# Low parts of every fourth gate and up weight chunk: a ScalarE activation and an accumulating DMA instead of a VectorE subtraction

## What is computed

```python
def swiglu(h, w_gate, w_up, w_down):
    return (jax.nn.silu(h @ w_gate) * (h @ w_up)) @ w_down

x = x + multiscale_pool_mixer(rms_norm(x, pool_norm), pool_w, pool_scale)   # layer 0
x = x + mla_layer_mixer(rms_norm(x, attn_norm), ...)                        # layer 1
x = x + swiglu(rms_norm(x, ffn_norm), w_gate, w_up, w_down)                 # both
```

## Time and profile before

| | |
|---|---|
| device time, 2 runs | 1771.51 and 1771.73 us, median 1771.62 |
| span of the profiled execution | 1769.1 us |
| TensorE matmul busy | 1761.5 us (100%) |
| VectorE busy | 1130.7 us (64%) |
| ScalarE busy | 914.3 us (52%) |
| GpSimd busy | 113.1 us (6%) |
| weights loaded by SyncE's queue | 327.03 MB, 55.5% of the 16 DMA engines' span |
| granted TensorE clock, mean | 0.999 |

### The profile page before, as it was taken

The page is one execution under the profiler, slowest core; times in us unless marked ns, Lnnn a source line. Parts: engine busy times, 40 slices in busy tenths (PEclk is TensorE's granted clock), DMA queues, the critical chain, the costliest instruction groups (busy, mean ns, idle before and its releaser), DMA issues.

```text
span 1769.1 us, 29325 instructions
## 1 busy us (share of the span) xinstructions
PE 1761.5 (100%) x10438; PEld 1564.0 (88%) x10438; DVE 1130.7 (64%) x1460; ACT 914.3 (52%) x1176; POOL 113.1 (6%) x132
## 2 busy tenths in 40 slices
PE   9999999999999999999999999999999999999998
PEld 6888888888888888889999888888888888888887
DVE  5766666556666666678997776666655566666554
ACT  6666664334444453456775466666533344445433
POOL 2100000000000001124111420000000000000000
PEclk9999999999999999999999999999999999999999
DMA  7555556545555566545445555555665455556642
GB/s 282 195 188 190 189 197 229 191 155 177 190 190 190 190 223 196 175 152 160 148 137 179 190 184 191 189 188 188 230 200 166 162 190 190 190 190 222 227 146 72
DMA packets 86017, 328.79 MB, mean 186 GB/s; under 512 B 9680, under 2 KB 11088, under 8 KB 85840
## 3 DMA queue, kind: packets, MB, share of 16 engines
q1 hardware_dynamic: 85680, 327.03, 55.5%
q10 hardware_dynamic: 288, 1.11, 0.2%
HBM read 326.01 MB, written 2.10 MB: 185 GB/s over the span
## 4 chain that ended last, share of the span: by engine, by line
PE 100%; DVE 0%; issue 0%; DVEq 0%; ACT 0%; POOL 0%; POOLq 0%
PE ps L435 58%; PE ps L436 31%; PE ps L505 2%; PE ps L443 1%; PE ps L445 1%; PE ps L444 1%; PE ps L799 1%; PE ps L798 1%; PE ps L797 1%; PE ps L633 0%; PE ps L632 0%; PE ps L631 0%; PE ps L685 0%; PE ps L493 0%; PE ps L705 0%; PE ps L706 0%
## 5 line engine op out<-in xcount | busy, mean ns | idle before, releaser
L1238 DVE TENSOR_TENSOR w_lo<-raw,w_hi 128x1024 fp32r<-128x1024 f32 (+2 forms) x564 | 736.0, 1308 | 419.1 <-ACT w_hi L850 416.9
L435 PE MATMUL ps<-xg,w_hi 128*128 128x512 f32 x2880 | 999.7, 390 | 0.0
L850 ACT ACTIVATE w_hi<-raw 128x1024 fp32r<-128x1024 f32 (+2 forms) x565 | 630.9, 1120 | 548.9 <-PE ps L436 533.2
L436 PE MATMUL ps<-xg,w_lo 128*128 128x256 f32 x2880 | 812.1, 282 | 0.0
L435 PEld LDWEIGHTS ps<-xg,w_hi 128*128 128x128 f32 x2880 | 540.5, 188 | 113.5 <-DVE w_lo L1238 0.3
L436 PEld LDWEIGHTS ps<-xg,w_lo 128*128 128x128 f32 x2880 | 544.3, 189 | 0.1
L435 PE MATMUL ps<-act,w_hi 128*128 128x512 f32 x1320 | 458.0, 390 | 0.0
L436 PE MATMUL ps<-act,w_lo 128*128 128x256 f32 x1320 | 372.2, 282 | 0.0
L435 PEld LDWEIGHTS ps<-act,w_hi 128*128 128x128 f32 x1320 | 247.7, 188 | 51.9
L436 PEld LDWEIGHTS ps<-act,w_lo 128*128 128x128 f32 x1320 | 249.5, 189 | 0.0
L1318 DVE TENSOR_TENSOR sums<-ps,cross 128x512 f32<-128x512 f32 x88 | 60.8, 691 | 93.1 <-ACT cross L928 93.1
(11 more groups left out here) (200 smaller groups left out, 1240.2 us busy)
## 6 DMA issues: line engine op xcount, KB each, us to landing
raw<-w_gate SPq DMA_DIRECT2D x176, 512.0 KB, 3.2
raw<-w_up SPq DMA_DIRECT2D x176, 512.0 KB, 3.2
raw<-w_down SPq DMA_DIRECT2D x120, 704.0 KB, 4.2
raw<-w_o SPq DMA_DIRECT2D x32, 512.0 KB, 3.2
raw<-w_last SPq DMA_DIRECT2D x11, 512.0 KB, 3.2
raw<-w_q_a SPq DMA_DIRECT2D x8, 512.0 KB, 3.2
raw<-w_kv_a SPq DMA_DIRECT2D x8, 512.0 KB, 3.3
raw<-w_q_nope SPq DMA_DIRECT2D x8, 512.0 KB, 3.2
```

The costliest lines, as they stand in the source:

```text
L435: pe.matmul(ps[:, bank, :], w_hi[:, s, j * P:(j + 1) * P], moving, start=start, stop=False)
L436: return pe.matmul(ps[:, bank, 0:SEQ], w_lo[:, s, j * P:(j + 1) * P], moving[:, 0:SEQ], start=False, stop=stop)
L850: nc.scalar.activation(dst, src, ACT.Copy).then_inc(hi_ready, 1)
L1238: nc.vector.tensor_tensor(lo, src, hi.bitcast(F32), ALU.subtract).then_inc(lo_ready, 1)
```

## The change

In each up stage, every fourth chunk from number 7 on (c = 7, 11, ..., 87, 21 chunks; `low_by_dma`), so 84 chunks in all, gets its low part in another way:
- ScalarE, after `w_hi`, runs a second activation on the same raw slot, scaled by -1, into the chunk's `w_lo` slot (it then holds the negated high part), and raises `negative_ready`.
- GpSimd waits for that and issues a DMA that adds the raw slot to the `w_lo` slot, SBUF to SBUF; it raises `low_landed` by 16. The function `lows(p)` issues the 21 of a stage. `lows(0)` and `lows(1)` stand before `stream_squares(2, "down1")`, `lows(2)` and `lows(3)` at the end of GpSimd's program.
- VectorE leaves these chunks out, and its next one raises `lo_ready` by 2, so that the count stays that of the chunks.
- TensorE (L455) and SyncE (L341) wait for `low_landed` where they waited for `lo_ready` of such a chunk.
- SyncE's and TensorE's loops get one body more written out ahead of them, SyncE's down loop its first body too, since the first waits of a stage follow another pattern. What is loaded and multiplied stays as it was.

```diff
+def low_by_dma(n):
+    for p in range(4):
+        c = n - CHUNK[f"up{p}"]
+        if 4 * FH > c >= 7:
+            return c % 4 == 3
+    return False
+
+def lows_landed(n):
+    for p in range(4):
+        c = n - CHUNK[f"up{p}"]
+        if 4 * FH > c >= 7:
+            return (FH - 1) * p + (c - 7) // 4 + 1
...
@@ SyncE, load
-                if before >= CHUNK["up0"]:
+                if low_by_dma(before):
+                    sp.wait_ge(low_landed, plus(16 * lows_landed(before), i, 32))
+                elif before >= CHUNK["up0"]:
                     sp.wait_ge(lo_ready, plus(made(before), i, BODY))
...
-                peel = 1 - half
+                peel = 2
...
-                with sp.Fori(0, tiles // 4) as i:
-                    for c in range(BODY):
+                for c in range(BODY):
+                    load(CHUNK[down] + c, w_down[(layer * 2 + half) * DT * 2 + c])
+                with sp.Fori(0, tiles // 4 - 1) as i:
+                    for c in range(BODY, 2 * BODY):
                         load(CHUNK[down] + c, w_down[plus((layer * 2 + half) * DT * 2 + c, i, BODY)], i)
...
@@ TensorE, long_tile
-                    pe.wait_ge(lo_ready, plus(made(n + c), i, BODY))
+                    if low_by_dma(n + c):
+                        pe.wait_ge(low_landed, plus(16 * lows_landed(n + c), i, 32))
+                    else:
+                        pe.wait_ge(lo_ready, plus(made(n + c), i, BODY))
...
@@ TensorE, ffn
                     long_tile(n0 + 6, t0 + 3, xg, TILES)
+                else:
+                    peel = 1
+                    for f in range(4):
+                        long_tile(n0 + 2 * f, t0 + f, xg, TILES)
...
@@ ScalarE, split
                 nc.scalar.activation(dst, src, ACT.Copy).then_inc(hi_ready, 1)
+                if low_by_dma(n):
+                    nc.scalar.activation(w_lo[:, n % SPLIT_SLOTS, 0:e], src, ACT.Copy,
+                                         scale=-1.0).then_inc(negative_ready, 1)
...
@@ VectorE, split
-                if n >= CHUNK["end"]:
+                if n >= CHUNK["end"] or low_by_dma(n):
                     return
...
-                nc.vector.tensor_tensor(lo, src, hi.bitcast(F32), ALU.subtract).then_inc(lo_ready, 1)
+                nc.vector.tensor_tensor(lo, src, hi.bitcast(F32), ALU.subtract).then_inc(
+                    lo_ready, 2 if low_by_dma(n - 1) else 1)
...
@@ GpSimd
+            def lows(p):
+                n = CHUNK[UPS[p]] + 7
+                def low(k, i=None):
+                    c = n + 4 * k
+                    gp.wait_ge(negative_ready, plus(lows_landed(c), i, 2))
+                    gp.dma_start(w_lo[:, c % SPLIT_SLOTS, 0:TILES * P].bitcast(F32),
+                                 raw[:, c % WEIGHT_SLOTS, 0:TILES * P],
+                                 accum_op=ALU.add).then_inc(low_landed, 16)
+                for k in range(FH - 1):
+                    low(k)
...
+            lows(0)
+            lows(1)
             stream_squares(2, "down1")
...
             stream_squares(5, "wo")
+            lows(2)
+            lows(3)
```

More of the change, by code:

```diff
@@ L257, in trunk @@
         lo_ready = sem("lo_ready")
+        negative_ready = sem("negative_ready")
+        low_landed = sem("low_landed")
         chunks_used = sem("chunks_used")
```

## The result

The changed kernel takes 1794.5 us (two runs, 1794.27 and 1794.71) against 1771.62: 22.9 us more, a ratio of 1.013 with a 95% interval of 1.0100 to 1.0159. It is inside the stated range, and on the forecast side of 2%, but the loss is 22.9 us where 8.4 were forecast, and it lies above the 1772 to 1786 us that case A alone allowed.

A forecast was written before the change was run, and what follows sets the result against it. The prediction took TensorE, running back to back, to bound the kernel. It added 7.9 us for two layer starts and 0.5 us for the clock to 1771.6, giving 1780 us (+0.5%), with a range of 1772 to 1900 us.

The forecast's parts named there:

- the forecast side of 2%: Whole kernel: a time within 2% of the kernel before, chance 0.53; slower 0.46, faster 0.01.
- case A: Low parts in time in steady state, D up to 5.35 us, only layer starts lose; 1772 to 1786 us, chance 0.49.
- TensorE bounds, so nothing can be gained: Whole kernel: TensorE's matmuls cover 1761.5 of 1769.1 us, so the ceiling for any gain is 7.6 us.
- ScalarE's delay is covered: Each feature tile: ScalarE's work behind the negation moves by 1.06 us, under a cover of 4.3 us; cost nothing.
- D = 1.6 + 2 x 1.57 = 4.75 us: GpSimd's DMA from issue to landing: fixed 1.6 us plus a 512 KB transfer of 1.57 us counted twice; budget 5.35 us.
- the rule of two reads: GpSimd's DMA: a reducing transfer pays for two reads per chunk and not for the addition, supporting the doubled 1.57 us.
- The layer starts: Chunk 7 of up0 and up2: TensorE stalls D - 0.8, so 3.95 us each, together 7.9 us.
- The clock's price: TensorE's clock might fall during the layer-start gaps: 0.5 us allowed over both, between 0 and 2.77 us each.
- No stall in 82 tiles: The other 82 tiles: stall is D - 5.35 if positive; with D at 4.75 us, none.
- adds up to a few tenths: Three loads released together reach into the next tile's accumulation; a D above 4.75 us adds up to a few tenths.
- the margin: Steady tiles: the DMA's 4.75 us lies inside the 5.35 us budget by 0.6 us only.
- B: A new wait once per feature tile, D = 5.35 to 6.9 us; 1861 us with three passes; chance 0.36.

The follow-up runs named there:

- e9: Changed kernel with chunks 7, 11, 83 and 87 of all up stages back on VectorE and the negation ahead of the high part on ScalarE; 1771.6 us.
- e5: Changed kernel with the 84 negations kept but GpSimd's DMAs gone, VectorE making every low part again; 1772.1 us.
- e3: Changed kernel with the loads of chunks 4 to 7 of each down stage held until the up stage's last accumulation has landed; 1791.7 us.
- e4: Changed kernel with ScalarE's negation ahead of the high part, so GpSimd's DMA starts 0.95 us earlier; 1791.0 us.
- e6: Changed kernel with the edits of e1, e3 and e4 in one, 82 accumulations staying; 1775.9 us.
- e1: Changed kernel with the low part of chunk 7 of up0 and up2 made on VectorE again, 82 chunks staying with the DMA; 1785.0 us.
- e7: Changed kernel with chunks 7, 11, 83 and 87 of all four up stages made on VectorE again, 68 accumulations staying; 1773.6 us.
- e2: Changed kernel with GpSimd's DMA a plain copy of the raw slot, the addition left out; 1778.9 us.
- e8: Changed kernel with half of each weight load of the up and down stages left out, the 84 accumulations unchanged; 1783.0 us.

## Why the prediction was right, and where it fell short

- **TensorE bounds, so nothing can be gained.** Right; e9 shows it with the other losses taken away.
- **ScalarE's delay is covered.** Right: 0.6 us in e5, inside its interval of nothing.
- **D = 1.6 + 2 x 1.57 = 4.75 us.** Right for an undisturbed one, and a little by luck. The shortest landing is 4.55. Its transfer took 2.73 against 3.15 (an SBUF copy holds the engines 1.29 us where the load from memory held 1.57), its fixed part 1.8 against 1.6, so the two terms err to opposite sides. The copy's fixed part is 2.9 - 1.29 = 1.6 us, that of SyncE's loads; a first byte 0.4 us later on GpSimd's path, which the prediction tried on top, doesn't show in it. One term was missing: from the negation's end to GpSimd's issue 0.29 us pass (0.04 in the sum), so issue and landing together are 4.84 against 4.79. As to the Trainium skill's pages: the rule of two reads in "Collectives: The Full Stack" ("The bandwidth ceiling: the fold count and why AG ≠ RS ≠ AR") agrees in size with 2.73 against 1.29. The estimate by the Trainium skill's "DMA: Bandwidth & Descriptors", "Anatomy of one DMA", was 4.4, 0.15 below the shortest landing here; for the copy it gives 2.0 + 1.2 = 3.2 against 2.9 measured.
- **The layer starts.** The gaps were to be 3.95 us each and are 4.11 and 3.92. The clock's price was mis-sized: 0.5 us allowed over both, with 2.77 each as a bound; measured 1.7 each. Term: 8.4 forecast, 11.7 measured. (The gaps are idle times; counted from matmul start to start each is 0.16 us more.)
- **No stall in 82 tiles.** This is the step that failed. The prediction saw that three loads would be released together and reach to where the next accumulation starts to move, wrote "adds up to a few tenths", and then entered nothing for it, though the margin was 0.6 us. The loads did bunch (three left at 1250.72 to 1251.91 us). In the steady tiles the few tenths were right in size: landings of 4.5 to 5.6 us, most inside the budget, 3.3 us lost. At the ends of the stages it never asked what the bunched loads are. They are down loads, 704 KB instead of 512: by an estimate from the 1.57 us of a 512 KB load four of them hold the engines 4 x 2.16 us, and with 2.73 for the accumulation that is 11.4 us of work for a tile of 11.09. The landing of chunk 87 rose to 5.8 to 6.5 us in all four stages, and e3 shows that the down loads did it. This doesn't cover all 8.2 us. Chunk 7 of up1 (5.9 us, and 8.1 in e4, 8.5 in e6) runs beside loads of 512 KB that left just before it; the prediction had put up1's start under the 82 without looking at its loads. And the 3.1 us at chunk 83 of up2 stay open, as told below.
- **The cases.** A and the foot of B were kept apart by D as one number. What came is neither: D has a spread, 4.5 to 8.2, with the threshold at about 5.25 inside it. 62 low parts came in time as in case A, 22 came late: the two of the layer starts, one that GpSimd issued late (below), and 19 that landed after 5.29 us or more. The measured 1794.5 lies between A's own upper bound of 1786 and the 1807 (2%) where B was to begin to count. It is inside the stated range only because that range was drawn to 1900 for B's sake, and B's mechanism, 82 waits of one size, didn't occur: the width of the range was right, by luck, and not its argument.

One more piece of the 8.2 us stays open. The 61st issue on GpSimd (chunk 79 of up2) came 1.05 us after its negation instead of 0.29:

```profile
1257.87 0.88 POOL L1774 DMA_DIRECT2D w_lo<-raw  x1 [10.99 <-issue]
...
1268.36 0.87 POOL L1774 DMA_DIRECT2D w_lo<-raw  x1 [9.62 <-ACT w_lo L882]
```

That low part landed just 0.2 us late, and SyncE's loads, which wait for it, left late and bunched. The next accumulation landed after 8.2 us and TensorE waited 2.8, the third row of the long gaps above. The chain that ended last, over that stretch:

```profile
1267.12 0.96 ACT w_lo L882
1268.08 0.28 issue
1268.36 8.24 DMA w_lo<-raw
1276.65 0.50 PE ps L458
```

The 61st issue is late by the same amount in all eight kernels with accumulations, also in those where another chunk is the 61st (e1, e6, e7, e9), so the lateness goes with the place in GpSimd's program. In e2, with a plain copy in the same place, it is absent. What makes that issue late stays open.

That it set off the 2.8 us gap seems likely by the order of events, but e3 and e4 speak against it as the whole cause. There the 61st issue is late too, the same four loads leave behind it, and the next accumulation lands after 5.4 us. The issues of this stretch, first in the changed kernel (1262.4 to 1276.6 us), then in e3 (1261.1 to 1272.4), with KB and median us to landing:

```profile
raw<-w_down SPq DMA_DIRECT2D x3, 704.0 KB, 8.6
w_lo<-raw POOLq DMA_DIRECT2D x1, 512.0 KB, 8.2
...
raw<-w_down SPq DMA_DIRECT2D x3, 704.0 KB, 6.0
w_lo<-raw POOLq DMA_DIRECT2D x1, 512.0 KB, 5.4
```

In the changed kernel the loads themselves were slower, already before the accumulation was issued. Why, no trace shows. With half the load traffic (e8) the place cost 0.1 us.

## What to carry to other kernels

When work moves from an engine to a DMA, draw its deadline chain with the DMA's time as a distribution, not a number: list what else the queues carry at each place where it runs, the largest and the nearest neighbours above all, and ask what the new wait makes the load queue do afterwards. Price the first and last iterations of a loop on their own; here they held 20 of the 23.7 us of the trace. And look first at whether the engine is the bound: here TensorE was, and 73 us off VectorE bought nothing.

## What the runs showed of the hardware

- An accumulating DMA from SBUF to SBUF of 512 KB, issued from GpSimd, holds the 16 engines 2.73 us and lands after 4.55 us when nothing else runs; a copy on the same path 1.29 and 2.9 us. The issue itself takes GpSimd 0.86 and 0.53 us.
- Its landing is sensitive to loads on the other queue: up to 8.2 us among 704 KB loads (changed kernel), and 8.5 us among three of 512 KB that left within 2.6 us before it (e6).
- TensorE's clock fell to half behind gaps of 3.26 and 1.84 us in e4 and not behind one of 3.08. The length alone doesn't decide it. In e2 it fell behind a gap of 2.31 us (granted clock 0.98 over the window with the gap, 0.59 over the one behind it), and in the changed kernel it stayed at 1.00 behind the one of 2.79. It may differ between executions of one kernel: of e2's five, the two shortest have a mean granted clock of 1.000, the other three 0.998. What decides it stays open. The two windows of e2:

```profile
1050.00:1053.00 3.00, 0.72 (x5) 0.36 (x3) 1.18 (x2) 2.99 (x5) 0.59 (x1) 0.98 0.43 175
1053.00:1057.00 4.00, 3.97 (x14) 3.41 (x15) 3.08 (x4) 1.34 (x2) 0.00 (x0) 0.59 0.69 224
```
- A kernel whose transfers collide has a spread of its own: the kernel before repeats within 1.5 us over all groups, e1 within 6.
